# Output projection that waits bank by bank and slice by slice, and starts with the second half of the sequence

## The reference

```python
def first_block(x, ...):
    xn = _rmsnorm(h, norm_mix_w[l])
    proj = xn @ w_in[l]
    q_a, k_a, v_a, qkv_g, z_g, a_g, b_g = jnp.split(proj, SPLIT_POINTS, axis=-1)
    attn = _windowed_gqa(q_a, k_a, v_a, band_bias, in_window, attn_sink[l])   # 8 blocks of 128 queries
    gdn = _gdn_mixer(qkv_g, z_g, a_g, b_g, ...)      # o = rmsnorm(o_fwd + o_bwd) * silu(z)
    h = h + jnp.concatenate([attn, gdn], axis=-1) @ w_out[l]      # the output projection
    hn = _rmsnorm(h, norm_ffn_w[l])
    h = h + jnp.square(jax.nn.relu(hn @ w_ffn_in[l])) @ w_ffn_out[l]
```

## Time and profile before

| | us |
|---|---|
| median of 3 runs | 2511.04 (2507.74 to 2512.07) |
| the profiled execution | 2507.24 |
| its span | 2505.4 |
| TensorE busy (matmuls) | 2380.4 (95%) |
| VectorE / ScalarE / GpSimd busy | 1422.1 / 1031.7 / 1042.1 |

### The profile page before, as it was taken

The page is one execution under the profiler, slowest core; times in us unless marked ns, Lnnn a source line. Parts: engine busy times, 40 slices in busy tenths (PEclk is TensorE's granted clock), DMA queues, the critical chain, the costliest instruction groups (busy, mean ns, idle before and its releaser), DMA issues. The chain is left out here.

```text
span 2505.4 us, 31190 instructions
## 1 busy us (share of the span) xinstructions
PE 2380.4 (95%) x11797; PEld 1901.5 (76%) x11797; DVE 1422.1 (57%) x1866; ACT 1031.7 (41%) x1748; POOL 1042.1 (42%) x647
## 2 busy tenths in 40 slices
PE   8999899997897999999999999999999999999986
PEld 6778678875675888878788777777777788877765
DVE  7754166554578545497766576666737541114753
ACT  5661234455234555543545343434333321015532
POOL 2112156444247666655777321212112341226553
PEclk9999999998898999999999999999999999999998
DMA  4113221121513444575543312111111452236562
GB/s 153 43 61 106 84 72 50 48 74 57 174 59 118 156 171 141 188 256 157 167 140 113 122 34 68 60 57 61 52 58 51 143 189 93 101 133 202 154 205 83
DMA packets 141730, 279.12 MB, mean 111 GB/s; under 512 B 26595, under 2 KB 36067, under 8 KB 141580
## 3 DMA queue, kind: packets, MB, share of 16 engines
q1 hardware_dynamic: 141580, 277.12, 33.6%
HBM read 200.44 MB, written 76.63 MB: 111 GB/s over the span
## 5 line engine op out<-in xcount | busy, mean ns | idle before, releaser
L1793 POOL TENSOR_TENSOR t<-t,t 128x512 fp32r<-128x512 f32 (+1 forms) x431 | 743.3, 1732 | 1174.2 <-ACT t L858 1155.7
L550 PE MATMUL bank<-t,t 128*128 128x512 f32 x1840 | 740.7, 403 | 25.6 <-ACT t L858 13.6
L552 PE MATMUL bank<-t,t 128*128 128x512 f32 x1840 | 721.7, 392 | 7.6 <-POOL t L1793 7.4
L554 PE MATMUL bank<-t,t 128*128 128x512 f32 x1840 | 720.8, 392 | 0.5 <-POOL t L1793 0.5
L858 ACT ACTIVATE t<-t 128x512 fp32r<-128x512 f32 (+1 forms) x581 | 398.5, 708 | 782.9 <-PE bank L554 387.4
L550 PEld LDWEIGHTS bank<-t,t 128*128 128x128 f32 x1840 | 347.7, 189 | 107.0 <-issue 35.5
L552 PEld LDWEIGHTS bank<-t,t 128*128 128x128 f32 x1840 | 348.2, 189 | 86.0 <-POOL t L1793 13.4
L554 PEld LDWEIGHTS bank<-t,t 128*128 128x128 f32 x1840 | 347.4, 189 | 75.2 <-POOL t L1793 0.9
L752 PE MATMUL bank<-t,t 128*128 128x512 f32 x896 | 352.2, 393 | 19.6 <-ACT t L858 18.8
L756 PE MATMUL bank<-t,t 128*128 128x512 f32 x896 | 352.3, 393 | 6.8 <-DVE t L1230 4.2
L754 PE MATMUL bank<-t,t 128*128 128x512 f32 x896 | 351.2, 392 | 2.8 <-POOL t L1793 2.8
(11 more groups left out here) (213 smaller groups left out, 2504.3 us busy)
## 6 DMA issues: line engine op xcount, KB each, us to landing
t<-in_w SPq DMA_DIRECT2D x87, 512.0 KB, 3.7
hid_scr<-t SPq DMA_DIRECT2D x112, 256.0 KB, 2.3
t<-hid_scr SPq DMA_DIRECT2D x112, 256.0 KB, 2.7
t<-in_wf SPq DMA_DIRECT2D x80, 256.0 KB, 3.4
g_scr<-t SPq DMA_DIRECT2D x36, 512.0 KB, 2.6
t<-g_scr SPq DMA_DIRECT2D x72, 256.0 KB, 3.4
t<-in_wf SPq DMA_DIRECT2D x35, 512.0 KB, 4.4
t<-in_wo SPq DMA_DIRECT2D x24, 512.0 KB, 3.7
```

What stands on the lines that cost most here:

```text
L550: e.matmul(ps[:, :], hi[:, w, :], XH[:, x, hs], start=k == 0, stop=False)
L552: e.matmul(ps[:, :], lo[:, w, :], XH[:, x, hs], start=False, stop=False)
L554: last = e.matmul(ps[:, :], hi[:, w, :], XL[:, x, hs], start=False, stop=k == j.nk - 1)
L1793: return e.tensor_tensor(out, x, high.bitcast(F32), ALU.subtract)
```

## The change

- **Banks.** The first use of P3's banks 0 to 2 waits for the preparation's last reads (`ltt`), that of bank 3 for the recurrence's last reads (`cO`, `gr`). Neither waits for attention.
- **Slices.** Each operand slice waits for what lay in its own place: `yah(., 0)` for `co(0, 7)`, the other copies for `co(1, 7)`, the low parts for what `y_low_free` names. `hx` waits for `qk` and `sc` of the last chunks.
- **Halves.** The first two tiles, and the loads and splits of the operands, begin with the second half; the first half's loads wait for the second half's copies and lows. Ranks are exchanged accordingly.
- **Attention.** Blocks 6 and 7 get rank 2 + n/8, their scaling rank -1, and transposes of a block are put behind those of the block before. Block 7's output is copied from the bank straight into yA (its last quarter), not by way of DRAM; the loads of the second half bring 384 columns only.

```diff
-        self.yA, self.yG = many(140, 2, 4, half), many(148, 2, 4, half)
+        self.yA, self.yG = at(140, [128, 4, 512]), many(148, 2, 4, half)
...
-        for m, half in [(0, 0), (1, 0), (0, 1), (1, 1)] + [(m, h) for m in range(2, 5) for h in range(2)] + [(m, h) for h in range(2) for m in range(5, 8)]:
+        for m, half in [(0, 1), (1, 1), (0, 0), (1, 0)] + [(m, h) for m in range(2, 5) for h in range(2)] + [(m, h) for h in range(2) for m in range(5, 8)]:
...
     def yah(h, j):
-        q.wait_ge(done("ya", h, j), *[done(*x) for x in K.p2_x])
-        copy(M.XH[:, j, HALF[h]], M.yA[j][:, :]).then_inc(*tick("yah", h, j))
+        q.wait_ge(done("ya", h, j), done("co", 1 if j else 0, 7))
+        if h:
+            q.wait_ge(done("ao", 7))
+        copy(M.XH[:, j, HALF[h]], M.yA[:, j, :]).then_inc(*tick("yah", h, j))
 
     def zh(h, j):
-        q.wait_ge(done("zm", h, j), *[done(*x) for x in K.p2_x])
+        q.wait_ge(done("zm", h, j), done("co", 1, 7))
...
-        e.tensor_copy(M.ao[:, :, :], v4(banks[7])).then_inc(*tick("ao", n))
+        if n == 7:
+            q.wait_ge(done("sc", 0, 7), done("sc", 1, 7))
+        out = M.yA[:, :, 384:512] if n == 7 else M.ao[:, :, :]
+        e.tensor_copy(out, v4(banks[7])).then_inc(*tick("ao", n))
...
-        q.wait_ge(done("yah", h, j), done("ya", h, j))
+        q.wait_ge(done("yah", h, j), done("ya", h, j), *[done(*x) for x in K.y_low_free(j)])
...
-        q.wait_ge(done("zh", h, j), done("zm", h, j))
+        q.wait_ge(done("zh", h, j), done("zm", h, j), *[done(*x) for x in K.y_low_free(4 + j)])
...
     def ya(h, j):
-        q.wait_ge(done("aout", 4 * h + 3), done("sc", 0, 7), done("sc", 1, 7))
-        if h:
-            q.wait_ge(done("yah", 0, j), done("yal", 0, j))
-        start(M.yA[j][:, :], M.attn_scr[j, :, HALF[h]], "ya", h, j)
+        q.wait_ge(done("aout", 6 if h else 3), done("sc", 0, 7), done("sc", 1, 7))
+        if h == 0:
+            q.wait_ge(done("yah", 1, j), done("yal", 1, j))
+        n = 384 if h else 512
+        start(M.yA[:, j, 0:n], M.attn_scr[j, :, 512 * h:512 * h + n], "ya", h, j)
...
     def hx(g, h):
-        q.wait_ge(*[done(*y) for y in K.p2_end])
+        q.wait_ge(*[done(x, d, 7) for x in ("qk", "sc") for d in range(2)])
...
-        self.p2_end = [("co", 0, 7), ("co", 1, 7), ("aout", 7)]
-        self.p2_x = [("co", 0, 7), ("co", 1, 7), ("atr", 7, 1)]
+        self.p2_end = [("co", 0, 7), ("co", 1, 7), ("ao", 7), ("aout", 6)]
...
+    def mix_bank_free(self, bank):
+        if bank == 3:
+            return [(x, d, 7) for d in range(2) for x in ("cO", "gr")]
+        return [("ltt", d, i, TOP) for d in range(2) for i in (6, 7)]
+
+    def y_low_free(self, k):
+
+        return [("co", 1, 7)] if k < 2 else [("am", g, 7, 3) for g in range(2)] if k < 5 else [("atr", 6, 2)]
...
-        r = 4 + n / 8
+        r = 4 + n / 8 if n < 6 else 2 + n / 8
...
-            add("pool", "ap", g, n, rank=r)
+            add("pool", "ap", g, n, rank=r if n < 6 else -1)
...
-            add("pe", "atr", n, s, rank=r, ring="attn", frees=[("atc", (g, n, s)) for g in range(2)])
+            add("pe", "atr", n, s, rank=r, ring="attn", frees=[("atc", (g, n, s)) for g in range(2)], behind=[("atr", (n - 1, K.blocks(n - 1) - 1))] if n else ())
...
-        add("dve", "ao", n, rank=5)
-        add("sp", "aout", n)
+        add("dve", "ao", n, rank=5 if n < 7 else 2)
+        if n < 7:
+            add("sp", "aout", n)
...
-            add("sp", "zl", h, j, rank=3 + h)
+            add("sp", "zl", h, j, rank=4 - h)
```

More of the change, by code:

```diff
@@ L1417, in ao @@
             q.wait_ge(done("aout", n - 1))
-        e.tensor_copy(M.ao[:, :, :], v4(banks[7])).then_inc(*tick("ao", n))
+        if n == 7:
+            q.wait_ge(done("sc", 0, 7), done("sc", 1, 7))
+        out = M.yA[:, :, 384:512] if n == 7 else M.ao[:, :, :]
+        e.tensor_copy(out, v4(banks[7])).then_inc(*tick("ao", n))
     def yal(h, j):
-        q.wait_ge(done("yah", h, j), done("ya", h, j))
-        low(M.XL[:, j, HALF[h]], M.yA[j][:, :], M.XH[:, j, HALF[h]]).then_inc(*tick("yal", h, j))
+        q.wait_ge(done("yah", h, j), done("ya", h, j), *[done(*x) for x in K.y_low_free(j)])
+        low(M.XL[:, j, HALF[h]], M.yA[:, j, :], M.XH[:, j, HALF[h]]).then_inc(*tick("yal", h, j))
     def zm(h, j):
@@ L2122, in ya @@
     def ya(h, j):
-        q.wait_ge(done("aout", 4 * h + 3), done("sc", 0, 7), done("sc", 1, 7))
-        if h:
-            q.wait_ge(done("yah", 0, j), done("yal", 0, j))
-        start(M.yA[j][:, :], M.attn_scr[j, :, HALF[h]], "ya", h, j)
+        q.wait_ge(done("aout", 6 if h else 3), done("sc", 0, 7), done("sc", 1, 7))
[3 more added lines that the diff above has]
+        start(M.yA[:, j, 0:n], M.attn_scr[j, :, 512 * h:512 * h + n], "ya", h, j)
     def zl(h, j):
         q.wait_ge(done("z_out", j), done("sc", 0, 7), done("sc", 1, 7))
-        if h:
-            q.wait_ge(done("zh", 0, j), done("zlo", 0, j))
+        if h == 0:
+            q.wait_ge(done("zh", 1, j), done("zlo", 1, j))
         start(M.yG[j][:, :], M.z_scr[j, :, HALF[h]], "zl", h, j)
     def hx(g, h):
-        q.wait_ge(*[done(*y) for y in K.p2_end])
+        q.wait_ge(*[done(x, d, 7) for x in ("qk", "sc") for d in range(2)])
         start(M.H[:, 2 * g:2 * g + 2, HALF[h]], A["xT"][:, 2 * g:2 * g + 2, HALF[h]], "hx", g, h)
@@ L2248, in bank_free @@
         p4 = {0: [("f6", 0)], 1: [("f6", 1)], 4: [("f7", 0)], 5: [("f7", 1)]}.get(j.bank)
-        return {"P1": [], "P3": self.p2_banks, "P4": p4, "P5": self.p4_end + [("ss", 0, 3, 7), ("ss", 1, 3, 7), ("stc", 3, 7, 3), ("vc", 3, 1)]}[B.stage_of[b]]
+        return {"P1": [], "P3": self.mix_bank_free(j.bank), "P4": p4, "P5": self.p4_end + [("ss", 0, 3, 7), ("ss", 1, 3, 7), ("stc", 3, 7, 3), ("vc", 3, 1)]}[B.stage_of[b]]
+    def mix_bank_free(self, bank):
[4 more added lines that the diff above has]
+        return [("co", 1, 7)] if k < 2 else [("am", g, 7, 3) for g in range(2)] if k < 5 else [("atr", 6, 2)]
     def weight_slot(self, n):
@@ L2607, in first_layer @@
             add("pe", "apv", n, s, rank=r)
-        add("dve", "ao", n, rank=5)
-        add("sp", "aout", n)
+        add("dve", "ao", n, rank=5 if n < 7 else 2)
+        if n < 7:
+            add("sp", "aout", n)
     for h in range(2):
         for j in range(4):
-            add("sp", "zl", h, j, rank=3 + h)
-            add("sp", "ya", h, j, rank=3 + h)
-            add("dve", "zm", h, j, rank=3 + h)
-            add("act", "zh", h, j, rank=3 + h)
-            add("pool", "zlo", h, j, rank=3 + h)
-            add("act", "yah", h, j, rank=3 + h)
-            add("dve", "yal", h, j, rank=3 + h)
+            add("sp", "zl", h, j, rank=4 - h)
+            add("sp", "ya", h, j, rank=4 - h)
+            add("dve", "zm", h, j, rank=4 - h)
+            add("act", "zh", h, j, rank=4 - h)
+            add("pool", "zlo", h, j, rank=4 - h)
+            add("act", "yah", h, j, rank=4 - h)
+            add("dve", "yal", h, j, rank=4 - h)
         for g in range(4):
-            add("sp", "hx", g, h, rank=5 + h)
+            add("sp", "hx", g, h, rank=6 - h)
     add("dve", "gg")
```

## The result

| | before | after |
|---|---|---|
| median of 6 runs, us | 2509.99 (2507.51 to 2514.39) | 2491.14 (2488.49 to 2493.19) |
| profiled execution, its span | 2507.24, 2505.4 | 2490.52, 2488.7 |
| projection's first product | 636.10 | 620.00 |
| projection's last product ends | 725.9 | 709.3 |

The ratio is 0.9926, with an interval of 0.9916 to 0.9936: 16 to 21 us. The forecast, 18.5 us off 2511.0, is a ratio of 0.9926 too. In the two profiled executions the span falls by 16.7 us, and 16.6 of these are there when the projection ends.

The account below looks back on a forecast made before the run. It took the seam between mixers and projection as the bound: about 22 us without work, the rest at half clock. 20.7 - 1.5 - 0.7 = 18.5 us off the 2511.0 median gave 2492.5 us; own range 2485 to 2499, 80% range 2484 to 2505.

Parts of the forecast that it names:

- part 2: Mixers' tail: attention blocks 6 and 7 go first; last recurrence product moves from 605.4 to 608.3 (+4.0 - 2.6 + 1.5).
- part 3: Projection start: with the second half first, tile 0 ends at 622.8 instead of 643.5, 20.7 us gained so far.
- Part 1: Projection's banks: no longer waiting for attention takes away the 7.9 us wait, leaving what follows dependent on operands alone.
- Part 4a: Tiles 0 and 1: waits between slices may leave products at half clock, 0 to 4.8 us lost, 1.5 taken.
- the rival: Projection tiles 0 and 1 both run at half clock: 4.8 us instead of 1.5, gain 15, time 2496; chance 0.05.
- Part 4b: First half's operand reloads before tile 2: stall of 0 to 3 us, taken as 0 because tile 1 covers them.
- Part 4c: VectorE has about 21 us of work in 22 us from 607: 0.7 us off for crowding, bounds 0 to 4.
- Small edits: Direct copy into yA, early residual loads (0 to 0.3 us, taken 0), GpSimd scaling first (delay 0 to 2.7 us).
- second rival (operand reload binds): Before tile 2, TensorE waits 6 us as reloads, z products and lows queue on single buffers: gain 12, 2499; chance 0.08.
- The rest moves as a block: From the projection's end on, order is unchanged and everything shifts together; the next seam stays 38 us long.
- The bare tail: Recurrence levels run without attention as filler: last product near 616, gain 11, time 2500; chance 0.13.
- The slower rival: Blocks 6 and 7 hold back pair 7's levels: tile 0 ends at 649, time 2516; decided past 629; chance 0.07.

Follow-up runs that it names:

- block 7 last: Changed kernel with attention block 6 still early but block 7 ranked behind all of the mixers' work (4.9): 2501.39 us, ratio 0.9968 to the kernel before.
- sums behind: Changed kernel with VectorE's four weight sums of the first pair placed behind direction 1's last recurrence add: 2492.86 us, ratio 0.9937 to the kernel before.
- lows first: Changed kernel with VectorE's first-pair weight sums behind both the last recurrence add and the second half's four attention lows: 2491.95 us, ratio 0.9930.
- weights behind: Changed kernel with ScalarE's first two projection weight copies placed behind attention block 7's bank copies: 2492.56 us, ratio 0.9935 to the kernel before.
- first half first: Changed kernel with the order of the halves as before in tiles, loads, waits and ranks: 2495.71 us, ratio 0.9951 to the kernel before.
- banks alone: Kernel before with only the projection banks' waits changed, from the whole list to what lay in each bank: 2506.66 us, ratio 0.9993.
- residual late: Changed kernel with the residual loads hx waiting for the mixers' end again: 2502.20 us, ratio 0.9967 to the kernel before.
- norm after lows: Changed kernel with VectorE's second-half attention lows ahead of direction 1's norm, the gains and the first-pair weight sums: 2493.91 us, ratio 0.9934.

## Why the prediction was right, and where it was not

The number was right to within the interval, in part by luck. By the terms of its own sum, from the kernel before's 725.9:

| term | forecast | measured |
|---|---|---|
| last recurrence product ends (part 2) | 608.3 | 614.9 |
| from there to the end of tile 0 (part 3) | 14.5 | 12.1 |
| fifteen tiles at the full pitch | 82.4 | 82.3 |
| clock and crowding (part 4) | 2.2 | 0 |
| projection ends | 707.4 | 709.3 |

The errors partly cancel: +6.6, -2.4, -0.1 and -2.2 make +1.9 us. With the recurrence's end at 614.9 the forecast's other terms would have given 714.0 and a gain of 11.9 us; the number came out because they were too dear by 4.7 us together.

Of the signs that it named, four came: block 7's copy before the last recurrence product, the clock back at 1.00 (from 625), no wait over 2 us before tile 2, a next seam of 38 us. Four did not, the last by little: the last recurrence product at 606 to 611 (614.9), the first product within 3 us of it (5.1), tile 0's end by 626 (627.0), the projection's end by 709 (709.3).

- **Part 1, banks: right in its mechanism.** The 7.94 us are gone, and what follows depends on operands. Restored in the changed kernel the list costs 3.4 us; alone its removal gave 1.3, hardly more than the noise of a trace. The same edit is worth either, depending on what stands behind it.
- **Part 2, the recurrence's end: mis-sized by 6.6 us.** Block 7's copy came before the last recurrence product, as forecast, and the wait of 2.64 us for ScalarE shrank to 0.78. The step that failed is the price of the move: it counted block 7's four groups and the bare levels, and nothing for block 6, whose rank changed as well. From 302 to the end of the last recurrence product TensorE is busy 285.5 of 303.4 us before and 293.4 of 312.9 after. The forecast had 4.0 us more work and 1.1 us less idle time (1.5 less 2.6); the trace has 7.9 us more work and 1.6 us more idle time. Of the 7.9, 4.3 are block 7's four groups (L729 and L739), priced rightly, and 1.0 is direction 0's norm sum (L710), which now comes first. The rest isn't assigned; part of it is the same number of products taking longer (L620, 178.8 instead of 176.8 us), in a kernel whose granted clock from 500 to 550 was 0.93 instead of 0.97. The kernel with block 7 last shows that block 6's rank puts one direction's chunk 6 back by 10 us, with the end at 614.4 even so. Why that direction loses and the other doesn't isn't separated further: the edits moved whole blocks only. TensorE also ran emptier there, 9.30 of 10.9 us busy from 590 to 600.9, where it had been full.
- **Part 3, tile 0: the order of the slices was wrong.** The forecast let the norm of direction 0 decide (614.4, then lows up to 622.8). That norm ended at 609.5, as direction 0 ended at 601.1 and not at 606.4: the forecast took it one group before direction 1, though the earlier trace rows had it 4.5 us ahead. So z's first two slices waited for direction 1's last product, not for their data. What stood before the first product was direction 1's norm sum, which the forecast called ready by 616 and which came at 618.9. It waited for an addition that VectorE made behind weight sums and products with z. That isn't a pure loss: of the four kernels that moved this start 2.4 to 3.5 us forward none ended sooner.
- **Part 4a, clock: 1.5 taken, next to nothing measured.** Three products of tile 0 run at half clock. The products behind the late start are dense. That the rival was near is seen in the kernels that start sooner: after waits of 2.0 to 2.6 us inside tile 0 (sums behind, lows first, weights behind) ten to thirteen products lie 0.43 us apart, about 2 to 2.6 us lost. The Trainium skill (TensorE: Matmul & The Clock Gate, "HAM oscillation") describes a TensorE that waits between bursts and falls back to half clock; the trace of those three agrees (0.50 from 625 to 630 with the sums behind). The rule alone doesn't tell when: the changed kernel's wait of 4.03 us was followed by three such products, and first half first's of 2.83 us, with one more of 0.37, by four.
- **Part 4b, reloads: the stall of 0 was right, its reason incomplete.** The landings were 3.4 and 4.2 us (3.1 and 5.0 in the earlier trace rows), and tile 1 covered them. With the residual loads just ahead of them they were 9.9 and 9.8.
- **Part 4c, crowding: 0.7 taken, none seen** in the projection's end; VectorE's queue shows up in the norm sum instead.
- **Small edits: `hx` priced at 0 to 0.3, worth 9.7 us.** The largest error of the forecast. It asked what the loads' own traffic costs where it was (640 to 650, nothing) and what it costs where it goes. It didn't ask what stands behind them in SyncE's queue in the new order: "the reloads and `hx` only swap places" is just the point. With their old condition they would have been the second rival (operand reload binds): gain 6.9 us by the projection's end (725.9 less 719.0), where that rival said 12.
- **The rest moves as a block: right.** The next seam is 38.1 us long before and after, and the wait in it 17.8 to 18.0 us in the experiments too.
- **The rivals.** The bare tail was given with last product near 616 and gain 11. The product did end past 614, the mark set for it, but the gain was 16.6, since z's slices had become ready meanwhile; a late end of one direction doesn't cost its whole delay when the projection begins with the half that the other completes. First half first shows the reverse: 4.8 us. The slower rival, ranks that starve the levels, was seen in part (block 6's groups ahead of chunk 6), at 11 us of delay in one direction, far from its point of 629.

So the gain belongs to parts that need each other. By what each costs when undone alone: the attention ranks 14.0 us (of these the scaling and the copy 3.7), the residual loads 9.7, the halves 4.8, the banks 3.4, the slices 0.1. They add up to 32 us, twice the gain, and the banks alone give 1.3 and not 3.4: each removes what would be last once the others are done. The 9.7 and the 14.0 include what the planner makes of the rest of the queue.

What stays open: whether some order of VectorE's list starts the projection at 617 and keeps both tile 0 and tile 2 fed (the four tried here don't), what block 7's priority costs without block 6's, and whether the residual loads could stay late behind the reloads. No run separates the directions in block 6's priority.

## What to carry to other kernels

Price a moved load by what stands behind it in its queue, in the new order, and not by the traffic at the place that it leaves or reaches. When a wait in front of products is taken away, list the operands' arrival times one by one: what counts is when the stage ends, and a start 2.4 to 3.2 us earlier with waits of 2 us inside ended 2.9 to 4.7 us later in three trials here. When priority is given to two blocks of work, price both, and look at each parallel chain by itself, since the one that loses can be far from the place of the move.

## What the runs showed of the hardware

- **Reloads behind large loads.** A 256 KB load landed 3.4 to 4.2 us after its issue in the changed kernel (medians of four), and 9.8 to 9.9 us behind eight loads of 512 KB on the same queue, while the DMA engines moved 396 GB/s:

```profile
625.00:630.00 5.00, 5.00 (x23) 4.14 (x23) 1.39 (x4) 1.14 (x3) 0.17 (x1) 1.00 1.06 396
```

  That stretch is from the kernel with the residual late; the changed kernel has a DMA share of 0.33 and 112 GB/s in the same one. The Trainium skill (DMA: Bandwidth & Descriptors, "Queues, rings and completion order") says that each DMA engine takes the descriptors of one ring in order; the trace agrees, though it can't tell this from a mere sharing of the engines.
- **VectorE beside a busy GpSimd.** An operation of 128x512 floats with both inputs in SBUF took 1.75 us (L1567 at 615.85) or 1.76 to 1.77 (the four lines shown of the kernel with the sums behind) while GpSimd made lows, and 0.69 otherwise (L1554 at 612.83). One with an input in a PSUM bank took 0.68 at 617.53 with GpSimd at work (L1371). By the Trainium skill (SBUF — State Buffer, "SBUF: two separate sides") the two engines lock each other out only where VectorE has two SBUF inputs (or a special mode); the trace agrees. In front of the lows the four sums took 3.8 us together, among them 4.9 (L1554 to L1567 of the two kernels).
- **The clock.** After waits of 1.23, 0.78 and 4.03 us three products were at half clock, and the granted clock was back at 1.00 from 625. After 1.82, 0.72 and 2.59 us, the last two among the products of tile 0 (sums behind), thirteen were. Five waits of 0.4 to 1.3 us in tiles 0 and 2, behind one of 1.82 (norm after lows), left it at 1.00.
